# A step of a head is given 1024 TensorE instructions, and its buffers are moved by 64 bytes

## The reference, cut to what matters

```python
def forget_gate(z, lb):
    k = (1.0 - lb) * jax.nn.sigmoid(-z)
    log_f = jnp.log(jnp.maximum(1.0 - k, F_MIN))
    return k, log_f

def chunk_scan(q, k, v, log_f, s0):
    def step(state, inp):
        qc, kc, vc, gc = inp
        bcum = jnp.cumsum(gc, axis=2)
        o_inter = jnp.einsum("bhtd,bhde->bhte", qc * jnp.exp(bcum), state)
        decay = jnp.where(tri, jnp.exp(rel), 0.0)
        scores = jnp.einsum("bhtd,bhsd,bhtsd->bhts", qc, kc, decay)
        o_intra = jnp.einsum("bhts,bhse->bhte", scores, vc)
        state = state * jnp.exp(b_end)[:, :, 0, :, None] + jnp.einsum(
            "bhsd,bhse->bhde", kc * jnp.exp(b_end - bcum), vc)
        return state, o_inter + o_intra

def mix_stream(h, w_in, ...):
    p = h @ w_in
    i_in, z_f, z_b, q_in, gate_a, u_f, gate_f = split_proj(p)
    ...
    o = o_f + flip(o_b)
```

## Time and profile before

| | us |
|---|---|
| median of 3 timed runs | 2167.99 |
| lowest and highest | 2167.6, 2169.31 |
| profiled execution, device time | 2162.09 |
| its span in the profile | 2160.3 |

### The profile page before, as it was taken

The page is one execution under the profiler, slowest core; times in us unless marked ns, Lnnn a source line. Parts: engine busy times, 40 slices in busy tenths (PEclk is TensorE's granted clock), DMA queues, the critical chain, the costliest instruction groups (busy, mean ns, idle before and its releaser), DMA issues.

```text
span 2160.3 us, 51162 instructions
## 1 busy us (share of the span) xinstructions
PE 2084.2 (96%) x21861; PEld 1812.0 (84%) x21861; DVE 1530.9 (71%) x3271; ACT 537.4 (25%) x964; POOL 75.1 (3%) x109
## 2 busy tenths in 40 slices
PE   5899999999999999999999999999998999999997
PEld 3799998899888888888888897898887887888886
DVE  4765854144878878787878878798998886565554
ACT  3621134212122212212221121222213443221121
POOL 0000101000000000000000000000000010000000
PEclk9899999999999999999999999999998999999999
DMA  9534555322424333342433333243335466445351
GB/s 380 183 123 144 171 165 148 112 81 94 133 84 138 107 100 120 104 126 94 123 102 117 101 107 123 91 139 110 106 114 202 164 250 241 159 133 182 129 185 55
DMA packets 226863, 299.08 MB, mean 138 GB/s; under 512 B 14996, under 2 KB 155952, under 8 KB 223309
## 3 DMA queue, kind: packets, MB, share of 16 engines
q1 hardware_dynamic: 142332, 178.38, 25.3%
q10 hardware_dynamic: 73952, 81.18, 11.2%
q0 software_dynamic: 10352, 36.25, 5.2%
HBM read 198.16 MB, written 97.59 MB: 137 GB/s over the span
## 4 chain that ended last, share of the span: by engine, by line
PE 89%; DVE 6%; DMA 2%; issue 1%; ACT 1%; SPq 1%; ACTq 0%; DVEq 0%; POOL 0%
PE all_bank L61 22%; PE all_bank L63 21%; PE all_bank L62 21%; PE all_bank L71 9%; PE all_bank L1553 3%; PE all_bank L1340 2%; PE all_bank L1509 2%; PE all_bank L1496 2%; PE all_bank L1546 1%; PE all_bank L1535 1%; PE all_bank L1339 1%; DVE hidden_h_lo L478 1%; PE all_bank L2680 1%; SPq L376 1%; DMA front_w_mod<-in_w_ada 1%
## 5 line engine op out<-in xcount | busy, mean ns | idle before, releaser
L61 PE MATMUL all_bank<-hidden_h_hi,head_hi 128*128 128x512 f32 x953 | 390.0, 409 | 3.0 <-issue 2.5
L62 PE MATMUL all_bank<-hidden_h_lo,head_hi 128*128 128x512 f32 x953 | 373.7, 392 | 3.9 <-issue 3.9
L63 PE MATMUL all_bank<-hidden_h_hi,head_lo 128*128 128x512 f32 x953 | 374.8, 393 | 2.7 <-issue 2.7
L1591 ACT ACTIVATE head_projected<-all_bank 128x512 f32<-128x512 f32 x148 | 88.7, 599 | 752.1 <-PE all_bank L63 592.0
L63 PEld LDWEIGHTS all_bank<-hidden_h_hi,head_lo 128*128 128x128 f32 x953 | 179.3, 188 | 44.4 <-issue 3.8
L61 PEld LDWEIGHTS all_bank<-hidden_h_hi,head_hi 128*128 128x128 f32 x953 | 179.5, 188 | 40.5 <-issue 3.5
L62 PEld LDWEIGHTS all_bank<-hidden_h_lo,head_hi 128*128 128x128 f32 x953 | 179.9, 189 | 35.5 <-issue 3.5
L1689 DVE RECIPROCAL head_inverse<-head_gate 128x448 f32<-128x448 f32 x64 | 185.1, 2927 | 0.0
L61 PE MATMUL all_bank<-front_hi,hidden_h_hi 128*128 128x256 f32 x512 | 143.7, 281 | 0.0
L62 PE MATMUL all_bank<-front_lo,hidden_h_hi 128*128 128x256 f32 x512 | 142.6, 279 | 0.0
L63 PE MATMUL all_bank<-front_hi,hidden_h_lo 128*128 128x256 f32 x512 | 142.6, 278 | 0.0
(11 more groups left out here) (315 smaller groups left out, 4701.4 us busy)
## 6 DMA issues: line engine op xcount, KB each, us to landing
head_raw<-in_w_in POOLq DMA_DIRECT2D x37, 512.0 KB, 5.0
head_value<-value_rows SPq DMA_DIRECT2D x64, 256.0 KB, 4.6
head_query<-piece_query SPq DMA_DIRECT2D x64, 256.0 KB, 5.6
head_out<-head_o ACTq DMA_DIRECT2D x64, 256.0 KB, 2.6
tail_o<-head_out SPq DMA_DIRECT2D x32, 512.0 KB, 5.9
front_raw<-in_w_in SPq DMA_DIRECT2D x19, 512.0 KB, 4.9
front_stage<-in_x SPq DMA_DIRECT2D x16, 512.0 KB, 7.5
front_w_mod<-in_w_ada SPq DMA_DIRECT2D x8, 1024.0 KB, 13.6
```

Source lines behind the costliest of these rows:

```text
L61: nc.tensor.matmul(out, st_hi, mv_hi, start=start, stop=False)
L62: nc.tensor.matmul(out, st_hi, mv_lo, start=False, stop=False)
L63: return nc.tensor.matmul(out, st_lo, mv_hi, start=False, stop=stop)
L1591: nc.scalar.activation(projected[unit % 2][:], ps_proj[unit % 2][:], PIECES[name][1], scale=PIECES[name][2]).then_inc(proj_copied, 1)
```

## The change

It does four things.

- `BY_COLUMNS` is filled for all steps. Heads 0 to 5: 8 row blocks (9 in head 0's first step), 8, 3, 3 in the four steps of a head; head 6: 16, 16, 11, 11; head 7: 16, 16, 15, 0. In all 234 instead of 231. Blocks of slot 0 take part too, all but k = 0.
- `EIGHT` drops slot 4 instead of slot 2: in heads 6 and 7 two slots stand between level 0 and level 1, and one between level 1 and level 2 (before: one and two).
- All buffers of the heads except `query_planes`, `key_planes` and `score` stand 64 bytes higher, so also `hi` and `lo`; the masks with them. `hc_hi` and `hc_lo` of `front` stand 64 bytes lower.
- Since `near` then overlaps another buffer of `front`, GpSimd waits for `front`'s last stores before it clears it, and with that before it issues the weights' DMA of head 0's second piece. VectorE waits for the clearing in step 2 instead of step 0.

```diff
-    hc_base = work + 60 * KB
+    hc_base = work + 60 * KB - HALF_LINE
...
-    EIGHT = (0, 1, 3, 4, 5, 7, 8, 9)
+    EIGHT = (0, 1, 2, 3, 5, 7, 8, 9)
...
-    BY_COLUMNS = {(0, 0): 20, **{(h, 0): 22 for h in range(1, HEADS - 1)}, (HEADS - 2, 1): 10, (HEADS - 2, 2): 15,
-                  (HEADS - 1, 0): 22, (HEADS - 1, 1): 22, (HEADS - 1, 2): 10}
+    BY_COLUMNS = {(h, g): (8 if h else 9, 8, 3, 3)[g] if h < HEADS - 2 else (16, 16, 11, 11)[g] if h == HEADS - 2 else (16, 16, 15, 0)[g]
+                  for h in range(HEADS) for g in range(NG)}
...
-    HC, VALUES, QUERY_W, RAW, GATE_W, OUT_ROWS, LITTLE = (work + i * KB for i in (60, 44, 28, 0, 8, 24, 76))
+    RAW = work
+    HC, VALUES, QUERY_W, GATE_W, OUT_ROWS, LITTLE = (work + HALF_LINE + i * KB for i in (60, 44, 28, 8, 24, 76))
...
         pool.wait_ge(handed.gate_out, TPG * DMA)
+        for sem in handed.stored:
+            pool.wait_ge(sem, handed.all_stored)
...
-                if k and slot and by_columns[h, g] > 0:
+                if k and by_columns[h, g] > 0:
...
             if n == 0:
+                v.wait_ge(handed.masks_in, DMA)
+            if n == NG // 2:
                 v.wait_ge(score_cleared, 2)
-                v.wait_ge(handed.masks_in, DMA)
```

More of the change, by code:

```diff
@@ L1459, in _ @@
     def _(pe):
-        by_columns = {(h, g): BY_COLUMNS.get((h, g), 0) for h in range(HEADS) for g in range(NG)}
+        by_columns = dict(BY_COLUMNS)
         def project_half(h, g, slot):
@@ L2749, in program @@
         with Room(nc, "hidden") as s:
-            masks = s.at("masks", [P, 2, MASKED, P], work + WORK, U8)
-            one_minus_lb = s.at("one_minus_lb", [P, 2, HEADS], work + WORK + 2 * MASKED * P)
+            masks = s.at("masks", [P, 2, MASKED, P], work + WORK + HALF_LINE, U8)
+            one_minus_lb = s.at("one_minus_lb", [P, 2, HEADS], work + WORK + HALF_LINE + 2 * MASKED * P)
             h_hi = [s.at(f"h_hi{g}", [P, KT, GRP], base + g * H_GROUP, F32R) for g in range(NG)]
```

## The result

The changed kernel takes 2152.53 us (median of 4 runs, 2150.28 to 2155.13) against 2167.8 us (4 runs, 2165.87 to 2169.31): a ratio of 0.993, 95% interval 0.9913 to 0.9948. Timed again on another chip it was 2149.89 against 2163.04, 0.9936 (0.9924 to 0.9948). So it is faster by 13 to 15 us. The forecast was 2151.7, its range 2145 to 2160.

A forecast was written before the change was run, and what follows sets the result against it. TensorE, busy 96% of the span, was taken as the bound. The terms -15.1 - 1.6 - 2.5 + 2.4 + 0.5 = -16.3 us took 2167.99 to 2151.7 us, range 2145 to 2160.

The forecast's parts named there:

- Stops that go: Ten TensorE stops in the heads, at late blocks of 256 instructions, vanish when the boundaries move: gain 15.1 us.
- the second boundary at 4.9 us: Behind slot 1 in the heads' steps, the step's second multiple of 256 instructions was taken to cause no stop.
- rival (a): The stops move to about 4.9 us into 19 steps, 0.5 us each: 9.5 us come back, 2161; chance 0.09.
- the prediction's own sign: Wrong if issue rows stay at L61 to L63, new ones stand behind slot 1 at 5 us, or products slow.
- SyncE's 1.5 MB: Loads that SyncE starts 1.3 us into a step, when near scores end, were taken to hold up instruction blocks.
- The threshold of 214 instructions: In heads 6 and 7, steps stall where the first 256-instruction boundary is at 214 to 221, not 179, 186 or 191.
- Pace: Heads' products of 512 columns take 6.5 us less, those in pairs of 256 take 4.9 us more: gain 1.6 us.
- Front and start: The context products of `front` gain 2.5 us; later weights for head 0's second piece cost 0.5 us.
- Slots of heads 6 and 7: In five steps there TensorE waits 0.3 to 0.6 us for VectorE's later operands: cost 2.4 us.
- (b): The holes belong to the time 2 us into a step, where loads start, and stay: 2166.8; chance 0.06.
- The sentence on the Trainium skill: By the skill, the fetch of 16 KiB instruction blocks is mostly hidden, so TensorE's ten stops would stay.
- (c): The 64 bytes make both operands' reads meet; heads' 512-column products slow to 0.240 us: 31 us, 2189; chance 0.04.

The follow-up runs named there:

- the counts alone: The changed tables (BY_COLUMNS, EIGHT) on the kernel before, every buffer left in place: 2152.51 us against 2163.91, ratio 0.9944.
- The kernel with the later loads: SyncE's loads of values and queries wait for level 1, on the changed kernel with 48 instructions more in the first step: 2229.41 us, ratio 1.0306.

## Why the prediction was right, point by point

**Stops that go.** Forecast -15.1 us for ten of them. All ten went, in every trace with the changed tables and their boundaries, and eight of them came back in the one with the old. For the six of step 1 the forecast was 11.8 us, the steps gave 11.1 (228.57 to 217.43) although eight row blocks more are done in pairs there. The four in level 1 went too; since in another trace of the old counts two of them were missing, their 3.3 us were one execution's.

**What came in their place** is where the reasoning fell short. I took the second boundary at 4.9 us as safe because three steps ran through there, and rival (a) priced what a late packet would cost. It happened in small, in heads' first steps alone: 1.8 us of idle time in one execution of the changed kernel, 0.4 in another, 7.6 in that of the counts alone. By the prediction's own sign, new rows behind slot 1 at 5 us, this part of it was wrong; and "issue" fell to 2.1 us, not under 2. The three steps it leaned on were no first steps, and the margin was misread a little: in step 1 of before TensorE goes on at 3.9 to 4.5 us, not 4.1 to 4.5. The prediction had also blamed SyncE's 1.5 MB for late blocks, and had them start at 1.3 us; the keys are issued from 0.9 us on, values and queries from 1.9. For a boundary passed at 0.7 us the runs clear values and queries, two thirds of it, and name the 512 KB of weights that GpSimd loads before a first step. The threshold of 214 instructions was in part that, since most of the steps of before with so late a first boundary were first steps. Not wholly: in head 6's step 2 and head 7's step 1 no weights were in flight, the boundary was passed at 1.1 us and the packet started only at 3.5 and 3.9. There SyncE's loads are the likely cause. The kernel with the later loads shows that they delay a packet asked for while they run, by 2.1 us on average; at that very place no run took them away, so for these two steps it is argued and not shown.

**Pace.** Forecast -1.6 us: -6.5 for 512 columns, +4.9 for pairs. Over all such products in the heads the mean distance of starts went from 229.6 to 228.4 ns, half of what I took from the tail, so 2850 of them gave 3.4 us. Pairs went from 116.2 to 119.5 ns, 4.6 us for 1404 matmuls, near the forecast. Together +1.2 instead of -1.6: the first term was mis-sized, because the 0.2290 read from one stretch was not the mean of the heads' products before, nor the 0.2267 that of after.

**Front and start.** Forecast -2.5 and +0.5. The first near product came at 505.5 and 502.7 us in two traces with the old offsets, at 499.6 to 503.2 in twelve with the new, mean 501.4: -2.7 us, with a scatter of 1 to 2. The context products went from 0.1199 to 0.1157 us on average, 4.2 ns each, which for 576 of them is 2.4 us. GpSimd issued the second piece's weights 1.1 us behind the first near product (502.34 against 501.21), where 1.9 was forecast, and TensorE waited nowhere for what follows from it.

**Slots of heads 6 and 7.** Forecast +2.4 us. L1538 waits for L1738, as foreseen, but in four steps and 0.9 us together, not five and 2.4. The net of both kernels' steps there is -0.3 us where -3.3 + 2.4 = -0.9 was forecast, and giving the slot back saved 1.3 us in the trace, so the term is nearer to 1.3 than to 2.4.

**The sum.** By these parts: -11.1 (step 1), -1.0 (steps 2 and 3), 0 to +2.5 (step 0), -0.3 (heads 6 and 7), -2.7 (front): -12.6 to -15.1, beside -13.1 and -15.3 timed and -16.3 forecast. The largest term was right in its place, its cause and nearly its size; the rest is small errors of both signs. That the median came within 1 us of the forecast is in part luck: the second timing has 3 us less of a gain.

**The rivals.** (b), holes that are not the fetch's, is refuted by the kernel in which 48 instructions put a stop into every step. The sentence on the Trainium skill that went with it ("Runtime: NRT & Kernel Launch", Instruction fetch mechanics) stands against the same runs: the blocks are of 256 instructions as it says, but here a block used up in less than 3.5 us isn't hidden. (c), products slowed by equal offsets, is refuted for 512 columns (0.2267) and holds in small for 256, where equal offsets cost 2 to 3 ns: by the means 119.6 against 116.2 ns with the old tables, 119.5 against 117.3 with the new. By the independent read ports of the Trainium skill ("SBUF — State Buffer", Who interferes with whom) there would be no difference at either width; at both there is one, of opposite sign.

## What to carry to other kernels

Where idle time is put down to "issue" inside a run of instructions that wait for nothing, count the engine's instructions between such places: if they are multiples of 256 apart, the instruction stream is late, and what helped here is to place the boundaries so that no 256 instructions are used up in less than about 3.5 us, or 4 to 6.4 where 512 KB of weights are in flight. Once a loop's body has a multiple of 256 instructions, one number at its start sets the phase for all turns: 48 instructions more cost 3.7%, 12 fewer changed nothing that the times could show. Keep large transfers from being in flight when a boundary is passed ahead of a burst of short instructions, and ask of each stop what is late behind it before you pay to remove it.

## What was not expected of the hardware

- From TensorE's passing a boundary among short products to the first instruction behind the next, a block took 3.2 to 3.9 us in 23 steps without weights in flight: 1.0 until its packet starts, about 1.1 for the packet, 1.4 until TensorE goes on. One block ahead is all that these stops show.
- A packet of instructions waits behind data: with 512 KB of weights in flight it started 2.0 to 4.6 us into the step instead of 1.7, with 1 MB of tables 4.1 to 5.1, and with 1 MB of values and queries a later one started 3.7 us behind the stop instead of 1.6.
- Products of 256 columns went at 0.116 to 0.117 us on average where moving and stationary operand begin at different halves of 128 bytes and at 0.120 where both begin at the same, while those of 512 columns went some 0.5% faster with the same (0.2284 us against 0.2296 on average). The products of `front` show it for 256 columns at both offsets. Why stays open.
- A wait that has long been met isn't free on TensorE: 24 products of 512 columns with two such instructions and a carried wait each took 0.14 us more than 24 without would by their pace.
